# A two-FFN decoder layer on eight cores: two norm transposes and a DMA queue changed

## The reference

```python
x = x + 0.5 * swiglu(rmsnorm(x, norm_ffn1), ffn1_gate, ffn1_up, ffn1_down)
h = rmsnorm(x, norm_mix)
proj = h @ w_in                     # (B,T,IN_DIM) = [gb | gc | u | p]
conv_out, new_conv = short_conv(gc * u, conv_hist, conv_w)
y_conv = gb * conv_out
y_pool, new_pool = multi_scale_pool(p, pool_hist, p0, pool_w, pool_scale)
x = x + jnp.concatenate([y_conv, y_pool], axis=-1) @ w_out
x = x + 0.5 * swiglu(rmsnorm(x, norm_ffn2), ffn2_gate, ffn2_up, ffn2_down)
return rmsnorm(x, norm_final), new_conv, new_pool
```

## Time and profile before

| | us |
|---|---|
| median of 3 runs | 1183.12 (1183.10 to 1184.17) |
| the profiled execution, its own time | 1184.01 |
| its span, slowest core (core 2) | 1182.5 |
| spans of all cores | 1180.0 to 1182.5 |
| TensorE busy | 1158.3 (98%) |
| VectorE busy | 603.7 (51%) |
| ScalarE busy | 275.1 (23%) |
| GpSimd busy | 172.5 (15%) |
| share of the chain that ended last: TensorE | 94% |

### The profile page before, as it was taken

How to read it: one execution, slowest core, us unless ns; L and a number is a source line. 1 busy time by engine, 2 the same in 40 slices (tenths; PEclk the granted TensorE clock), 3 DMA queues, 4 the chain that set the end, 5 groups by cost and what they waited for, 6 DMA issues and landing times.

```text
span 1182.5 us, 19766 instructions; the slowest of 8 cores (1180.0 to 1182.5 us)
## 1 busy us (share of the span) xinstructions
PE 1158.3 (98%) x6761; PEld 627.8 (53%) x6872; DVE 603.7 (51%) x951; ACT 275.1 (23%) x639; POOL 172.5 (15%) x293
## 2 busy tenths in 40 slices
PE   7999999999999999999999999999999999999997
PEld 6745445445445454476777744445445445445455
DVE  4744344344344455777876756334334344344476
ACT  4611111111111112445554421111111111111234
POOL 5310000000000001335543510000000000000013
PEclk9999999999999999999999999999999999999999
DMA  9976402403103108382321637502402402400123
GB/s 199 238 113 148 72 1 38 71 1 54 27 1 54 28 5 130 63 126 37 55 46 25 112 53 122 78 1 34 74 1 36 72 1 39 69 1 1 47 114 144
DMA packets 71330, 74.80 MB, mean 63 GB/s; under 512 B 45760, under 2 KB 45760, under 8 KB 71232
## 3 DMA queue, kind: packets, MB, share of 16 engines
q0 software_dynamic: 21504, 43.52, 23.3%
q1 hardware_dynamic: 49440, 29.74, 9.9%
q10 hardware_dynamic: 288, 0.27, 0.1%
HBM read 93.63 MB, written 10.03 MB: 88 GB/s over the span
## 4 chain that ended last, share of the span: by engine, by line
PE 94%; issue 2%; POOL 1%; DMA 1%; DVE 1%; ACT 1%; POOLq 0%; DVEq 0%; ACTq 0%
PE ps L523 54%; PE ps L554 27%; PE ps L630 6%; PE ps L808 4%; PE ps L653 2%; DMA ring<-ffn_gate 1%; POOL scr L695 0%; POOL wsum L690 0%; PE ps L415 0%; DVE xres L815 0%; DVE hp L391 0%; ACT junk L378 0%; POOL ring L327 0%; ACT ring L793 0%; DVE scr L711 0%
## 5 line engine op out<-in xcount | busy, mean ns | idle before, releaser
L523 PE MATMUL ps<-hT,ring 128*128 128x512 bf16 (+2 forms) x3713 | 676.9, 334 | 4.3 <-DVE hp L391 0.6
L523 PEld LDWEIGHTS ps<-hT,ring 128*128 128x128 bf16 x3776 | 337.9, 98 | 326.9 <-issue 1.4
L534 DVE TENSOR_TENSOR scr<-scr,ps 128x512 bf16<-128x512 f32 (+2 forms) x236 | 135.5, 576 | 449.0 <-PE ps L523 442.4
L554 PE MATMUL ps<-ring,scr 128*128 128x512 bf16 x1452 | 349.5, 379 | 1.9
L561 DVE SCALAR_TENSOR_TENSOR xres<-ps,xres 128x512 f32<-128x512 f32 x406 | 274.7, 689 | 51.0 <-PE ps L554 45.4
L532 ACT ACTIVATE scr<-ps 128x512 f32<-128x512 f32 (+2 forms) x236 | 119.7, 508 | 752.7 <-PE ps L523 743.2
L554 PEld LDWEIGHTS ps<-ring,scr 128*128 128x128 bf16 x1488 | 143.9, 98 | 162.5
L630 PE MATMUL ps<-hT,ring 128*128 128x256 bf16 (+1 forms) x864 | 93.9, 267 | 0.6 <-DVE wsum L716 0.4
L630 PEld LDWEIGHTS ps<-hT,ring 128*128 128x128 bf16 x864 | 80.6, 98 | 12.1 <-issue 0.7
L378 ACT ACTIVATE junk<-xres 128x1024 bf16<-128x1024 f32 x67 | 70.6, 1054 | 69.0 <-DVE xres L561 37.9
L327 POOL DMA_DIRECT2D ring<-ffn_gate x15 | 10.8, 719 | 509.2 <-PE ps L523 467.5
(11 more groups left out here) (78 smaller groups left out, 313.2 us busy)
## 6 DMA issues: line engine op xcount, KB each, us to landing
ring<-ffn_gate POOLq DMA_DIRECT2D x8, 1024.0 KB, 11.6
ring<-ffn_up POOLq DMA_DIRECT2D x8, 1024.0 KB, 16.3
ring<-ffn_down POOLq DMA_DIRECT2D x8, 1024.0 KB, 10.3
yp<-xres SPq DMA_DIRECT2D x16, 512.0 KB, 2.6
xres<-xp SPq DMA_DIRECT2D x11, 512.0 KB, 9.8
ring<-w_in POOLq DMA_DIRECT2D x4, 1024.0 KB, 12.9
xres<-xp POOLq DMA_DIRECT2D x5, 512.0 KB, 15.8
ring<-w_out POOLq DMA_DIRECT2D x2, 1024.0 KB, 18.9
```

The lines of the kernel that those rows point to most:

```text
L523: ins = e.matmul(ps[bank][:, 0:N], lhsT=ring_gu(slot[0])[:, slot[1] + jj, kc, :], rhs=hT[:, kc, tok0:tok0 + N], start=(kc == 0), stop=(kc ...
L534: P.op("dve", lambda e: e.tensor_tensor(out=aT[:, buf, jj, off:off + N], in0=sg[:, sk, 0:N], in1=ps[ub][:, 0:N], op=ALU.mult), reads=[("sg ...
L554: ins = e.matmul(ps[db][:, 0:512], lhsT=aT[:, buf, jj, ti * 128:(ti + 1) * 128], rhs=ring_dn(ds)[:, do + jj, dh * 512:(dh + 1) * 512], sta ...
```

## The change

- `PE_TILES` goes from 10 to 8: tiles 8 and 9 of the first norm are transposed by DMA, no longer on TensorE.
- The DMA transposes of tiles 8 to 11 in the first norm are issued by ScalarE; tile 12's, on SP, waits until all four have landed.
- The norm row is loaded as one row of 1024 numbers into one partition, and spread with two products of a row of ones (512 columns each) instead of eight of 128 columns.
- GpSimd's queue has 24 semaphores, ScalarE's 6.
- A load that GpSimd issues is put by the scheduler where the queue would be free for 60 ns (`ISSUE_GAP`), so operations that are ready then go first.
- In the mixing stage the folds and convolutions of the first steps are recorded in another order, and the first output product waits for the last W_in product recorded.
- Tile 15's multiplication by the norm row is two halves; the second comes after the last silu multiplication.

```diff
-PE_TILES = 10
+ISSUE_GAP = 60
+PE_TILES = 8
...
+        o.idle = FILL_GAP if lazy else idle
...
-            t, _, o = min(((max(free[e], at[o]) + (FILL_GAP if o.lazy else 0), o.gidx, o)
+            t, _, o = min(((max(free[e], at[o]) + o.idle, o.gidx, o)
...
-        last_t[0] = P.op("sp", transpose_dma, reads=[("hp", k)], writes=[("hT", tt)], dma=True, c=1240, nbytes=262144)
+        on_act = f1 and tt < 12
+        last_t[0] = P.op("act" if on_act else "sp", transpose_dma, reads=[("hp", k)], writes=[("hT", tt)], dma=True,
+                         c=1240, nbytes=262144, after=tuple(act_t) if tt == 12 else ())
+        if on_act:
+            act_t.append(last_t[0])
...
-        def spread(e, h=h):
-            ins = None
-            for q in range(4):
-                ins = e.matmul(ps[6 + h][:, q * 128:(q + 1) * 128],
-                               lhsT=gcol[:, 4 * h + q:4 * h + q + 1].to_broadcast([128, 128]),
-                               rhs=idf[:, :], start=True, stop=True)
-            return ins
-        P.op("pe", spread, reads=[("gcol",), ("idf",)], writes=[("ps", 6 + h)], c=1800)
+        P.op("pe", lambda e, h=h: e.matmul(ps[6 + h][:, 0:512], lhsT=ones[:, :], rhs=grow[:, h * 512:(h + 1) * 512],
+                                           start=True, stop=True),
+             reads=[("ones",), ("grow",)], writes=[("ps", 6 + h)], c=1890)
...
-            for q in range(1 if tt == 15 else 2):
-                w = 1024 if tt == 15 else 512
-                P.op("dve" if tt == 15 else "pool", lambda e, q=q, w=w: e.tensor_tensor(
-                    out=buf[:, q * w:(q + 1) * w], in0=xres[:, tt, q * w:(q + 1) * w],
-                    in1=gbc[:, 1, q * w:(q + 1) * w], op=ALU.mult),
-                    reads=[("x", tt, q), ("x", tt, 1), ("gbc", 1)][:3 if tt == 15 else 1] + [("gbc", 1)],
-                    writes=[("xs", i, q)] + ([("xs", i, 1)] if tt == 15 else []), c=1220 if tt == 15 else 1280)
+            for q in range(2):
+                P.op("dve" if tt == 15 else "pool", lambda e, q=q: e.tensor_tensor(
+                    out=buf[:, q * 512:(q + 1) * 512], in0=xres[:, tt, q * 512:(q + 1) * 512],
+                    in1=gbc[:, 1, q * 512:(q + 1) * 512], op=ALU.mult),
+                    reads=[("x", tt, q), ("gbc", 1)], writes=[("xs", i, q)], c=690 if tt == 15 else 1280,
+                    after=(prod[0],) if tt == 15 and q else ())
...
+        mix_conv(g, 1)
         if gi_ == 1:
             fold_pool(2)
-        mix_conv(g, 1)
-        if gi_ == 1:
+            mix_conv(g, 2)
             fold_pool(3)
             mix_pool_fin(g)
-            mix_conv(g, 2)
-        mix_wout(before)
+            mix_conv(g, 3)
+        mix_wout(before, (last_win[0],) if gi_ == 1 else ())
...
-            "pool": [es.enter_context(nc.semaphore("dq_pool%d" % i)) for i in range(12)],
+            "pool": [es.enter_context(nc.semaphore("dq_pool%d" % i)) for i in range(24)],
...
-            "act": [es.enter_context(nc.semaphore("dq_act%d" % i)) for i in range(2)], "pe": [], "dve": [],
+            "act": [es.enter_context(nc.semaphore("dq_act%d" % i)) for i in range(6)], "pe": [], "dve": [],
```

More of the change, by code:

```diff
@@ L41 @@
     __slots__ = ("eng", "fn", "deps", "eidx", "sig", "sem", "val", "dma", "waits", "gidx", "extra_waits",
-                 "cost", "nbytes", "done", "chain", "lazy", "stop")
+                 "cost", "nbytes", "done", "chain", "lazy", "stop", "idle")
 class Prog:
@@ L52, in __init__, with op @@
         self.res = {}
-    def op(self, eng, fn, reads=(), writes=(), dma=False, after=(), c=100, nbytes=0, chain=False, lazy=False, stop=False):
+    def op(self, eng, fn, reads=(), writes=(), dma=False, after=(), c=100, nbytes=0, chain=False, lazy=False, stop=False, idle=0):
         o = Op()
         o.lazy, o.stop = lazy, stop
+        o.idle = FILL_GAP if lazy else idle
         o.chain = chain
@@ L264, in build_nc @@
     stt = nc.alloc_sbuf_tensor("stt", [128, 32], F32)
-    gcol = SCR[:, 3424:3432]
+    ones = SCR[0:1, 3424:3552]
+    grow = wsum[0:1, :, :].rearrange("p a b -> p (a b)")
     nhalf = nc.alloc_sbuf_tensor("nhalf", [128, 1], F32)
@@ L328, in load_unit @@
                     writes=[("ring", slot, off + jj) for jj in range(nb)],
-                    after=after, c=600 if nb == 1 else 900, nbytes=nb * 128 * 4096, chain=True)
+                    after=after, c=600 if nb == 1 else 900, nbytes=nb * 128 * 4096, chain=True,
+                    idle=ISSUE_GAP if nb == 1 else 0)
     def load_ffn_part(f, b, pch, slot, off=0, after=()):
@@ L360, in load_x @@
         xload[tt] = P.op(eng, lambda e: e.dma_start(out=xres[:, tt, :], in_=src),
-                         writes=[("x", tt, 0), ("x", tt, 1)], dma=True, after=after, c=420 if eng == "sp" else 600, nbytes=128 * 4096, chain=True)
+                         writes=[("x", tt, 0), ("x", tt, 1)], dma=True, after=after, c=420 if eng == "sp" else 600, nbytes=128 * 4096, chain=True,
+                         idle=0 if eng == "sp" else ISSUE_GAP)
     def load_gbc(i, g_ap):
@@ L395, in build_nc, with norm_B @@
     last_t = [None]
-    def norm_B(tt):
+    act_t = []
+    def norm_B(tt, f1):
         k = hp_of[tt]
@@ L426, in norm_B_pe, with norm @@
                  reads=[("ps", bank)], writes=[("hT", tt)], c=1230)
-    def norm(tt, gi, pe=False):
+    def norm(tt, gi, pe=False, f1=False):
         nA1(tt)
@@ L431, in norm @@
         nA3(tt, gi)
-        (norm_B_pe if pe else norm_B)(tt)
+        norm_B_pe(tt) if pe else norm_B(tt, f1)
     load_x(0)
-    P.op("act", lambda e: e.dma_start(out=gcol[:, :], in_=norm_ffn1[:, :]),
-         writes=[("gcol",)], dma=True, c=420, nbytes=4096)
+    P.op("act", lambda e: e.dma_start(out=grow[:, :], in_=norm_ffn1.rearrange("(o d) -> o d", o=1)),
+         writes=[("grow",)], dma=True, c=420, nbytes=4096)
+    P.op("pool", lambda e: e.memset(ones[:, :], 1.0), writes=[("ones",)], c=90)
     load_x(1)
@@ L505, in build_nc @@
     silu = [None]
+    prod = [None]
     def ffn_GU_ops(f, b, grp, buf, off=0, hold=99):
@@ L533, in emit @@
                      reads=[("ps", gb)], writes=[("sg", sk)], c=act_c(N))
-                P.op("dve", lambda e: e.tensor_tensor(out=aT[:, buf, jj, off:off + N], in0=sg[:, sk, 0:N],
+                prod[0] = P.op("dve", lambda e: e.tensor_tensor(out=aT[:, buf, jj, off:off + N], in0=sg[:, sk, 0:N],
                                                       in1=ps[ub][:, 0:N], op=ALU.mult),
@@ L795, in fold_pool, with mix_wout @@
                 reads=[("ps", 5 + dh)], writes=[("ring", slot, gi)], c=act_c(512))
-    def mix_wout(g):
+    def mix_wout(g, after=()):
         G = mix_geom(g)
@@ L812, in mix_wout @@
                 P.op("pe", pe_fn, reads=[("ring", mix_slots["o%d" % h], j) for h in range(2) for j in range(4)] +
-                     [("mixT", mb, c) for c in range(8)], writes=[("ps", ob)], c=8 * 216)
+                     [("mixT", mb, c) for c in range(8)], writes=[("ps", ob)], c=8 * 216, after=after)
                 xs_ = xres[:, tt, dh * 512:(dh + 1) * 512]
@@ L912, in finish_last @@
                              reads=[("xl", 1), ("xl", 2)], dma=True, c=420, nbytes=128 * 2048))
-    P.alias([("poolb", gi) for gi in range(4)], [("iot",), ("gcol",)])
+    P.alias([("F", gi) for gi in range(4)], [("grow",)])
+    P.alias([("poolb", gi) for gi in range(4)], [("iot",), ("ones",)])
     pre1 = {}
     for g in range(1, len(FG)):
-        pre1[(0, g - 1)] = [lambda tt=tt: norm(tt, 0, pe=tt < PE_TILES) for tt in FG[g][2]]
+        pre1[(0, g - 1)] = [lambda tt=tt: norm(tt, 0, pe=tt < PE_TILES, f1=True) for tt in FG[g][2]]
     def slots1(b):
```

6 lines of the change are left out of this document (3 added, 3 removed).

## The result

The changed kernel is slower. Its time is 1.0044 times that of the kernel before, 95% interval 1.0032 to 1.0056, which is 5.2 us on 1183.1, or 1188.3 us. The profiled execution took 1188.86 us, its span is 1187.2 us (core 4). The forecast was 1180.6 us with a range of 1178.5 to 1183.5, and 1188.3 lies outside it.

What follows compares the result with a forecast made beforehand. TensorE, busy for 98% of the span, was taken to bound the kernel. Terms 0.9 + 0.7 - 0.3 + 0.8 + 0.4 = 2.5 us took the median 1183.1 to 1180.6 us, range 1178.5 to 1183.5.

Steps and rivals of the forecast that it cites:

- Four transposes on ScalarE: First block: DMA transposes of tiles 8 to 11 delay ScalarE's squares and silus; 0.3 us lost, ends 0 and 1.5.
- The rival of the held queue: A transpose keeps ScalarE's queue until it lands, 3.3 instead of 1.24 us each; 7.9 us lost, 1188.5 us; chance 9%.
- Two transposes leave TensorE: First block: tiles 8 and 9 no longer occupy TensorE, 0.45 us each; 0.9 us won.
- The start moves up: First block: no load waits for semaphores, statistics precede GpSimd's loads, tile 6's square moves; 0.7 us won, ends 0 and 2.3.
- the start does not move: Rival: landings set the start everywhere, so the 0.7 us are gone; 1181.3 to 1181.8 us; chance 18%.
- the case that it moves whole: Rival: core 2's start becomes like core 0's, with 2.3 us won in place of 0.7; 1179.0 us; chance 17%.
- No load waits: Start, GpSimd's queue: with 24 semaphores no load waits for a weight block's landing, where one sat 1.14 us.
- The mixing order: Mixing stage: reordering covers TensorE's second and third waits, the first stays; 0.8 us won, ends 1.3 and nothing.
- the 8% rival: Mixing stage: the waits only move; 1181.4 us, no difference to be told; chance 8%.
- Tile 15 in halves: End: only a 0.65 us half precedes the silu multiplications, so TensorE's wait goes; 0.4 us won, ends 0 and 0.4.
- Norm row 0: Start: an earlier norm row gains 0 us, since the work after tiles 0 to 2 waits for tile 3 and loads.
- tile 12's wait 0: First block: tile 12's transpose waits for all four, going out at 57 to 58 us; hidden, 0 us.

## Why the prediction was wrong

- **Four transposes on ScalarE** was the step that failed. It set 0.3 us lost, ends 0 to 1.5, and it is 5.6 us in the mean span. "Add up ScalarE's order" took 1.23 us for each from the earlier trace rows. Those seven were issued on core 2 from 51.0 us on, when the last loads were landing, while the two that the change puts ahead go out at 46 and 48, in the stretch where the same prediction read a DMA share of 0.97. The first two took 6.77 us on core 4, not 2.5. The silus stood behind them as the sum had it, and so TensorE was late by what the issues were over. The trace of the kernel before had a hint on other cores, where the first transposes go out sooner than on core 2. The second one, core 3:

```profile
L401 SPq DMA_TRANSPOSE hT<-hp x1: 2090/2090/2090, 50.8 to 50.8; - x1
```

Cores 0 and 5 had 1.88 and 2.10 us, and all three issues ended as the last tile landed, within 0.4 us.
- **The clock** had no term. Waits of TensorE of 2.6 to 4.5 us in sum went with time at 1.2 GHz on seven of eight cores, about 7 us of it on core 4. Filling the gap took between a fifth and nearly a half of the loss away.
- **The rival of the held queue** had 9% and 1188.5 us, and 1188.3 was measured. The mechanism was nearly right and the sum right by luck. It said that every transpose is held until it lands; in truth the first goes out, only the second is held, and only while the loads run. That is 4.3 us more than reckoned, under the 5.3 that the rival wanted over its four, and the clock made up for it. Its sum also counts the 0.3 us of the central case beside its own 7.9: without them it is 1188.2, and the bound 5.6 in place of 5.3. It was put at 9% with the argument that the seven on SP went out 2.3 us apart. The same rows could not speak for the loads' stretch, and the range should have reached to that rival. (The range's worst end also gives tile 15's halves 0.2 us where their own worst end is 0: 1183.7, not 1183.5.)
- **Two transposes leave TensorE**, 0.9 us: with all on SP's queue, 8 and 9 by DMA against 8 and 9 on TensorE is -0.2 against +0.1, so 0.3 us. The start seems to be set by landings, so that most of what TensorE is spared there turns into waiting.
- **The start moves up**, 0.7 us: 0. What tile 6 had of air before the change did not arrive at the third group. The rival "the start does not move" (18%) was right on this term, and what the Trainium skill says of small pieces, taken for the case that it moves whole, bears on the row alone.
- **No load waits**: true for landings of weights, which are gone from GpSimd's waits, but the loads now wait for statistics, and the new order costs 1.2 us where the norm row comes late. "The statistics stand ahead of the loads" was written down as a gain, without asking what is queued behind a statistic.
- **The mixing order**, 0.8 us: 0.1 to 0.3. The waits moved, as the 8% rival had it.
- **Tile 15 in halves**, 0.4 us won: in the changed kernel TensorE's wait grew by 0.1 us in the mean of the cores and the end by 0.3, and with all transposes on SP the half cost 0.3 to 0.4 us. The 0.38 us to be won were those of core 2; six of the eight cores had 0.17 before. The step "only a half (0.65 us) stands before them" left out that GpSimd's products of tile 14 run at the same time.
- **Norm row 0, tile 12's wait 0, next block's weights 0** hold. On core 4 tile 12's transpose goes out at 64.5 us, not at 57 to 58, the weights at 78.12 instead of 70.25, and still TensorE waits for nothing from 66 to 500 us.

The changed kernel stands at +4.6 us and its transposes alone at +5.6, so the other parts seem to give 1.0 there, against nothing when they stand alone. In the one profiled execution of each the lower clock between 54 and 62 us took 1.9 us of the changed kernel and 2.7 of the other, mean of the cores, which would be most of that difference. It rests on four and five executions and stays open. So does what inside a queue holds the second transpose.

## What to carry to other kernels

Before a DMA is moved to the queue of an engine that computes, ask how full the DMA engines are at the moment it will be issued, and take its issue time from rows of that stretch, on every core, or bound it by the landing of the last load there; a short issue time from a quiet stretch says nothing. A wait of TensorE of two to four microseconds in a busy kernel can cost up to nearly double (on core 4 4.3 us of waits and 3.2 of clock), since the granted clock can fall behind it. A wait that is taken away is worth only what the next limit leaves, so in a start set by landings neither an earlier norm row nor fewer transposes bring more than some tenths.

## What the runs showed of the hardware

- Issue time of a transpose (128x1024, bf16) depends on traffic: mostly 1.2 to 1.3 us with the loads done; while they run 1.3 to 2.7 for the first and 3.5 to 5.2 for a second right behind it, until the last load lands (changed kernel, eight cores), and 2.9 to 4.7 for the second on SP's queue. Landing: 3.1 us against 5.7 to 8.3.
- In the profiled execution the granted clock fell to half in or behind TensorE's wait on seven of eight cores: on core 4 for 6.8 us from 55.6 on, on five cores for 3.4 us, which costs 1.7. On core 7, which waited for 1.80 and 1.12 us, it did not fall; on core 1, with 1.98 and 0.58, it did.
- A 128x512 product on VectorE took 1.68 us beside a GpSimd product on SBUF, 0.69 alone: it ended 0.54 us after GpSimd's.
- The norm row in one piece was ready by 3.5 to 3.6 us, in 128 pieces by 5.17 to 7.32.
